# Latent attention unrolled over four head pairs, with the next pair's projections inside the second pass and the outputs taken by halves

## The reference

```python
q = (_rmsnorm(c_q, q_norm) @ w_uq).reshape(B, L, MLA_HEADS, MLA_QK_DIM)          # rank 256 -> 8 x (64 + 32)
q = jnp.concatenate([q[..., :64], _rope(q[..., 64:], cos, sin)], axis=-1)
kv = (_rmsnorm(c_kv, kv_norm) @ w_ukv).reshape(B, L, MLA_HEADS, 64 + 64)          # rank 128
k_nope, mv = kv[..., :64], kv[..., 64:]
k_rope = _rope(k_r[:, :, None, :], cos, sin)                                      # one for all heads
k = jnp.concatenate([k_nope, jnp.broadcast_to(k_rope, (B, L, MLA_HEADS, 32))], axis=-1)
mla = _block_sweep(q, k, mv, 96 ** -0.5, ..., mla_mask)                           # softmax(q k) v, chunk-causal
mla = mla.reshape(B, L, MLA_WIDTH) * jax.nn.silu(m_gate)
y = jnp.concatenate([fox, mla], axis=-1) @ w_out
```

## Time and profile before

| | |
|---|---|
| runs, median of 3 (lowest to highest) | 3171.92 us (3170.37 to 3172.45) |
| the profiled execution | 3178.12 us, its span 3176.3 us |
| TensorE busy | 3044.0 us, 96% of the span |
| VectorE, ScalarE, GpSimd busy | 1526.0, 947.3, 762.2 us |
| mean granted clock of TensorE | 0.975 |
| stages LAT and MLA | 2620.3 to 3064.2 us of the span |

### The profile page before, as it was taken

One profiled execution on the slowest core, in us unless ns is written; L12 is line 12 of the kernel. 1 busy time (PEld: TensorE's weight loads), 2 busy tenths in 40 slices (PEclk: granted clock), 3 DMA queues, 4 the chain that ended last, 5 costly groups with the idle time before them and its releaser, 6 DMA issues.

```text
span 3176.3 us, 38630 instructions
## 1 busy us (share of the span) xinstructions
PE 3044.0 (96%) x14225; PEld 2339.0 (74%) x14225; DVE 1526.0 (48%) x1761; ACT 947.3 (30%) x1502; POOL 762.2 (24%) x486
## 2 busy tenths in 40 slices
PE   6999999999999999999999999999999999999998
PEld 5887875556777777778888888777777777666666
DVE  6464554555344343453344334441455554566654
ACT  4323235666200022322221122221143431333441
POOL 5302112223233312133333333312110101101025
PEclk8999999999999999999999999999899999999999
DMA  5201000000211101011111111102100001000023
GB/s 199 67 21 34 28 21 14 14 14 18 85 50 43 49 28 34 21 47 47 46 46 46 46 46 48 51 30 84 28 21 15 8 11 30 5 2 7 1 100 119
DMA packets 162998, 128.83 MB, mean 41 GB/s; under 512 B 14880, under 2 KB 146688, under 8 KB 162608
## 3 DMA queue, kind: packets, MB, share of 16 engines
q1 hardware_dynamic: 161456, 118.55, 12.3%
q10 hardware_dynamic: 1408, 8.50, 0.7%
HBM read 114.20 MB, written 12.65 MB: 40 GB/s over the span
## 4 chain that ended last, share of the span: by engine, by line
PE 66%; DVE 5%; issue 2%; ACT 1%; DMA 1%; SPq 0%; POOL 0%; DVEq 0%; ACTq 0%; POOLq 0%
PE ps L675 16%; PE ps L677 15%; PE ps L676 15%; PE ps L2345 7%; PE ps L594 2%; PE ps L2404 2%; PE ps L2405 1%; PE ps L2406 1%; PE ps L2489 1%; PE ps L2491 1%; PE ps L2490 1%; PE ps L671 1%; DVE dF L1883 1%; PE ps L612 1%; PE ps L2302 0%
## 5 line engine op out<-in xcount | busy, mean ns | idle before, releaser
L675 PE MATMUL ps<-NH,w_high 128*128 128x512 f32 (+1 forms) x2048 | 801.8, 391 | 31.3 <-POOL w_low L962 8.0
L676 PE MATMUL ps<-NL,w_high 128*128 128x512 f32 (+1 forms) x2048 | 802.7, 392 | 0.0
L677 PE MATMUL ps<-NH,w_low 128*128 128x512 f32 (+1 forms) x2048 | 799.0, 390 | 0.0
L960 POOL CAST w_high<-w_raw 128x1024 fp32r<-128x1024 f32 x193 | 212.1, 1099 | 2233.3 <-PE ps L677 1203.7
L962 POOL TENSOR_TENSOR w_low<-w_raw,w_high 128x1024 fp32r<-128x1024 f32 x193 | 485.0, 2513 | 15.4
L675 PEld LDWEIGHTS ps<-NH,w_high 128*128 128x128 f32 x2048 | 389.9, 190 | 129.8 <-issue 25.7
L677 PEld LDWEIGHTS ps<-NH,w_low 128*128 128x128 f32 x2048 | 390.4, 191 | 85.0
L676 PEld LDWEIGHTS ps<-NL,w_high 128*128 128x128 f32 x2048 | 389.6, 190 | 85.7
L737 DVE TENSOR_TENSOR hT<-hT,ps 128x1024 f32<-128x1024 f32 x168 | 205.1, 1221 | 250.1 <-PE ps L677 250.1
L1306 ACT ACTIVATE probs_high<-ps 128x512 fp32r<-128x512 f32 (+4 forms) x224 | 112.8, 504 | 228.5 <-PE ps L2345 189.6
L1851 DVE TENSOR_TENSOR probs_low<-probs,probs_high 128x512 fp32r<-128x512 f32 (+4 forms) x224 | 133.2, 599 | 86.5 <-ACT probs L1308 81.7
(11 more groups left out here) (355 smaller groups left out, 5108.2 us busy)
## 6 DMA issues: line engine op xcount, KB each, us to landing
w_raw<-in_w_in SPq DMA_DIRECT2D x69, 512.0 KB, 3.8
w_raw<-in_w_up SPq DMA_DIRECT2D x44, 512.0 KB, 3.8
w_raw<-in_w_out SPq DMA_DIRECT2D x24, 512.0 KB, 3.5
w_raw<-in_w_down SPq DMA_DIRECT2D x22, 512.0 KB, 3.7
w_raw<-in_w_xkv SPq DMA_DIRECT2D x8, 512.0 KB, 5.9
x_in<-in_x SPq DMA_DIRECT2D x8, 512.0 KB, 9.3
residual_spill<-hT SPq DMA_DIRECT2D x1, 4096.0 KB, 13.6
hT<-residual_spill ACTq DMA_DIRECT2D x1, 4096.0 KB, 13.0
```

What stands on the lines that cost most here:

```text
L675: nc.tensor.matmul(o, wh, xh, start=start, stop=False)
L676: nc.tensor.matmul(o, wh, xl, start=False, stop=False)
L677: return nc.tensor.matmul(o, wl, xh, start=False, stop=stop)
L960: nc.gpsimd.tensor_copy(WH[slot][:, :], w_raw[slot][:, :]).then_inc(w_high, 1)
```

## The change

- The loop over MLA is written out: four pairs in the program, no loop; the order has no units for the values of the meta tokens (`pair_order(False)`, 56 units).
- A pair's projections are packed over its two heads into five jobs (`m_project`): QN (queries without rope, 64 + 64 rows, 12 matmuls), QP (rope part and its half-swapped copy, 12), KN (keys, 6), KVM (meta keys and meta values), VN (values by tokens: the latent is the stationary operand, 8 x 3 matmuls of 128 columns; no transposes). They use one pair of banks (`SP_`); both heads' outputs use the other (`SU`).
- The next pair's jobs are issued within the second pass, ahead of blocks 1, 6, 10, 16 and 21 (`M_JOB`). ScalarE's high parts follow its exponentials 3, 10, 12 and 18 (`M_HIGH`), VectorE's rotation stands at 8 and 9, its low parts at 3, 4, 11 to 14 and 19. The values are split after the second pass and in the next first pass. Queries and keys have two sets of buffers in `NH` and `NL`; their constant rows are filled once by GpSimd, ahead of the split of pair 1's first tile.
- Numerators and denominators are taken by head and half (after blocks 9, 17, 23 and the last), the reciprocal by quarters of 256 columns (`m_invert`: two at blocks 24 and 26, two in the next first pass), the product by halves (`m_finish`).
- Of the 61 + 4 x 64 fillers of LAT and MLA none is left; the 50 ahead of OUT stay.
- LAT projects the query latents first, then keys and values, then the rope key; the sums and rows of the norms lie between matmuls of the later projections (`between`), with their own buffers; the rotated key is made behind the norms. The rope table is loaded without a wait for the last FOX pair.
- SP loads a pair's weights in 4 + 8 parts in place of 4 + 4.

```diff
-            st_mla = Stage(st_nkvm, 2, list("xwxwxoo") * 2, 116, 4)
+            st_mla = Stage(st_nkvm, 4, [], MLA_UNITS, 2)
...
+        M_JOB = {1: QN, 6: QP, 10: KN, 16: KVM, 21: VN}
+        M_HIGH = {3: QN, 10: QP, 12: KN, 18: KVM}
+        M_ROTATION = {8: 0, 9: 1}
+        M_LOW = {3: [(QN, 0)], 4: [(QN, 1)], 11: [(QP, 0)], 12: [(QP, 1)], 13: [(KN, 0)], 14: [(KN, 1)], 19: [(KVM, 0), (KVM, 1)]}
+        M_TAKEN = {9: (0, 0), 17: (0, 1), 23: (1, 0)}
...
+            dense(pe, LAT, 0, 0, 0, NH, NL)
+            dense(pe, LAT, 0, 1, 1, NH, NL)
+            wait_bank(pe, LAT, 0, 0)
+            dense(pe, LAT, 0, 2, 2, NH, NL, meta=(bank[LAT.bank(0)], 0, l_meta), between={
+                (0, 4): lambda: norm_sums(pe, "q", 0), (HALF, 0): lambda: norm_sums(pe, "q", 1),
+                (HALF, 6): lambda: norm_rows(pe, "q")})
+            dense(pe, LAT, 0, 3, 3, NH, NL, between={
+                (0, 4): lambda: norm_sums(pe, "kv", 0), (HALF, 1): rope_meta, (HALF, 3): lambda: norm_rows(pe, "kv"),
+                (HALF, 6): lambda: norm_sums(pe, "kvm", 0)})
...
+            m_project(0, QN)
+            norm_rows(pe, "kvm")
+            for j in (QP, KN, KVM, VN):
+                m_project(0, j)
+            for pm in range(4):
+                pb, s = pm + 4, pm % 2
+                pe.wait_ge(m_qk, pm + 1)
...
+                    elif what[0] == "p2":
+                        _, h, half, j, n, unit = what
+                        if pm < 3 and n in M_JOB:
+                            m_project(pm + 1, M_JOB[n])
+                        pe.wait_ge(p_rows[h], pb * 32 + 32)
+                        wait_bank(pe, MLA, pm, unit)
...
+            def m_project(pm, j):
+                o = m_slot(pm, j)
...
+                else:
+                    for t in range(NT):
+                        ts = slice(t * P, (t + 1) * P)
+                        mm = three(o[:, ts], kvH[:, 0, ts], kvL[:, 0, ts], WH[s1][:, late], WL[s1][:, late], True, True)
+                    mm.then_inc(tile_done, 1)
...
+            def m_denominators(pm, h, half):
+                hs = slice(half * HALF, (half + 1) * HALF)
+                dve.wait_ge(p_pv, (pm + 4) * 28 + 14 * h + (14 if half else 5) + 4)
+                nc.vector.tensor_copy(dF[HD * h:HD * h + HD, hs], pair[SU][HD * (1 - h):HD * (1 - h) + HD, hs]).then_inc(m_den, 1)
+            def m_invert(pm, quarter):
+                qs = slice(quarter * 256, (quarter + 1) * 256)
+                dve.wait_ge(m_den, 4 * pm + 3 + quarter // 2)
+                nc.vector.reciprocal(dF[:, qs], dF[:, qs]).then_inc(m_rec, 1)
...
+                    elif what[0] == "p2":
+                        n = what[4]
+                        if n in M_TAKEN:
+                            m_denominators(pm, *M_TAKEN[n])
+                        if n in (24, 26):
+                            m_invert(pm, (n - 24) // 2)
+                        if n == 27:
+                            m_finish(pm, 0)
...
+                        if pm and seen in (2, 4):
+                            m_invert(pm - 1, 2 + seen // 4)
+                        if pm and seen == 6:
+                            m_finish(pm - 1, 1)
+                        if seen == 8:
+                            m_values_low(pm)
```

More of the change, by code:

```diff
@@ L191, in pair_order @@
         out.append(("pv", 1) + blocks[m % 14] + (m,))
-    assert unit == 58
+    assert unit == (58 if metas else 56)
     return out
 LAG = 3
+MLA_UNITS = 56
+QN, QP, KN, KVM, VN = range(5)
 ROWS = 126
@@ L615, in norm_pe @@
             mm.then_inc(n_row, 1)
-            if name in UPDATED:
-                busy(bank[1], 14)
         def norm_dve(dve, name):
@@ L993, in _, with one @@
                         nc.gpsimd.tensor_copy(spH[n % 3][:, c0:HALF], xS[n % 4][:, c0:HALF]).then_inc(s_hi, 1)
-            tiles(ahead + 12, NTILES)
+            third = MLA.w0 + 2
+            def one(n):
+                pool.wait_ge(w_landed[n % 2], 16 * (n // 2 + 1))
+                pool.wait_ge(tile_done, n - 1)
+                split(n % 2, n)
+            assert third % 2 == 1
+            tiles(ahead + 12, third - 1)
+            one(third - 1)
+            pool.wait_ge(tile_done, LAT.tile(0, 4))
+            pool.wait_ge(w_ready, third)
+            for s_ in range(2):
+                for h in range(2):
+                    for n, (to, value) in enumerate(((KH, 1.0), (KL, 0.0), (QH, 0.0), (QL, 0.0))):
+                        pool.wait_ge(m_filled, 8 * s_ + 4 * h + n) if s_ + h + n else None
+                        nc.gpsimd.memset(to[s_][h][96:P, :].bitcast(F32), value).then_inc(m_filled, 1)
+            pool.wait_ge(m_filled, 16)
+            one(third)
+            tiles(third + 1, NTILES)
             if NTILES % 2:
@@ new lines, in latent @@
+            def latent(k, c):
+                wait_done(act, LAT, 0, k)
+                nc.scalar.activation(lat[:, c, 0:T], pair[LAT.slot(k)], ACT.Copy).then_inc(job_free[LAT.slot(k)], 1)
+            act.wait_ge(p_pv, 4 * 28 + 4)
+            latent(0, 0)
+            act.wait_ge(p_o, 5)
+            wait_freed(act, LAT, 0, 0)
+            norm_square(act, "q", 0)
+            latent(1, 1)
+            wait_freed(act, LAT, 0, 1)
+            norm_square(act, "q", 1)
+            norm_std(act, "q")
@@ new lines, in _ @@
+            latent(2, 2)
+            act.wait_ge(l_meta, 1)
+            nc.scalar.activation(lat[:, 2, T:T + META], bank[LAT.bank(0)][:, 0:META], ACT.Copy).then_inc(l_mfree, 1)
+            wait_freed(act, LAT, 0, 2)
+            norm_square(act, "kv", 0)
+            for c in range(2):
+                norm_high(act, "q", c)
+            norm_std(act, "kv")
+            act.wait_ge(l_mfree, 1)
+            norm_square(act, "kvm", 0)
+            norm_high(act, "kv", 0)
+            norm_std(act, "kvm")
@@ new lines, in k_rope @@
+            def k_rope(src, done, lo, n, parts, free):
+                done()
+                nc.vector.tensor_tensor(parts[0][0:32, 0:n], src[0:32, 0:n], rope_m[0:32, lo:lo + n], ALU.mult)
+                nc.vector.tensor_tensor(parts[1][0:32, 0:n], src[HD:96, 0:n], rope_m[HD:96, lo:lo + n], ALU.mult)\
+                    .then_inc(free, 1)
+            dve.wait_ge(rope2_in, 48)
+            dve.wait_ge(n_lo, NORM["kvm"][2] + 1)
+            k_rope(pair[LAT.slot(3)], lambda: wait_done(dve, LAT, 0, 3), 0, T, ud, job_free[LAT.slot(3)])
@@ L2431, in _ @@
                               m_own, m_ownT, J + 3, J + 4, ready, 8)
-            for x in range(4):
-                if x < 2:
-                    wait_bank(pe, LAT, 0, x)
-                dense(pe, LAT, 0, x, x, NH, NL, meta=(bank[LAT.bank(x)], 0, unit_done) if x < 2 else None)
-            for name, n in (("q", 24), ("kv", 15), ("kvm", 22)):
-                norm_pe(pe, name)
-                wait_pair(pe, MLA, 0, 0)
-                busy(pair[MLA.slot(0)][:, 0:HALF], n)
-            pe.wait_ge(n_lo, NORM["kvm"][2] + 1)
@@ new lines, in rope_meta @@
+            def rope_meta():
+                slot = (LAT.w0 + 3) % 2
+                pe.wait_ge(l_mfree, 1)
+                for c in range(C):
+                    mm = three(bank[LAT.bank(0)][:, 0:META], WH[slot][:, c * P:(c + 1) * P], WL[slot][:, c * P:(c + 1) * P],
+                               NH[:, c, T:T + META], NL[:, c, T:T + META], c == 0, c == C - 1)
+                mm.then_inc(unit_done, 1)
+            dense(pe, LAT, 0, 0, 0, NH, NL)
+            dense(pe, LAT, 0, 1, 1, NH, NL)
```

568 lines of the change are left out of this document (389 added, 179 removed).

## The result

The changed kernel takes 3124.4 us (median of 4 runs, 3116.2 to 3126.4) against 3172.2 us of the kernel before, run beside it (4 runs, 3170.4 to 3176.2). The ratio is 0.9843, 95% interval 0.9823 to 0.9863: faster by 1.6%, 47.8 us. The forecast was 3117 us, 55 us faster, with a range of 3098 to 3141.

The account below looks back on a forecast made before the run. VectorE was taken to bound the interlude between pairs (25.97 of 27.7 us), TensorE the second pass. Savings of 35.3 (periods) + 1 (last pair) + 19 (latents and pair 0) = 55 us gave 3171.9 - 55 = 3117 us, range 3098 to 3141.

Parts of the forecast that it names:

- (c): Rival: recurring waits hold TensorE at 1.2 GHz through the three second passes; slower, up to 3266 us; chance 0.05.
- (b): Rival: stalls and clock loss at their upper ends, period 84.5 us, prologue saving 14; 30 saved, 3142 us; chance 0.17.
- Second pass: Second pass with the next pair's projections inside: 39.5 + 10.3 = 49.8 us, before stalls and splits.
- The projections: Next pair's five jobs on TensorE in the second pass: 10.3 us added.
- The stalls: Second pass: TensorE waits from inserted VectorE and ScalarE steps, at masked blocks and reciprocal quarters; 2 us (nothing to 5).
- the splits: GpSimd weight splits in second passes of pairs 0, 1 and 2, blocking VectorE's low parts: 2.5 us each pass (1 to 5).
- First pass: First pass stays 21.7 us (18.5 to 24): VectorE's lag replaces the clock's 3.5 us loss.
- The period: From first pass to first pass: 21.7 + 49.8 + 2 + 2.5 + 2 = 78.0 us; 35.3 saved over three.
- Pair 3: Last pair, no projections and no split in its way: 21.7 + 39.5 + 1 = 62.2 us against 63.2, 1 saved.
- Latents and pair 0: Stretch before pair 0's first pass: projections end at 62 us, pass starts at about 90; 19 us saved (12 to 25).
- The loop's turn: Unrolling saves the loop's turn inside the second period: 3 us, already counted in the 269.3.
- The constants on GpSimd: GpSimd's 16 constant fills before pair 0: 1 us each, hidden.

Follow-up runs that it names:

- Run 1: Changed kernel with the next pair's projections and their splitting behind the second pass instead of inside it: 3167.3 us, ratio 0.9984 to the kernel before.
- run 4: Changed kernel plus fillers at blocks 23 to 26 of the second pass, ahead of four early first-pass units and ahead of block 0: 3119.7 us, ratio 0.9834.
- 9: Changed kernel without reciprocal quarters 0 and 1 and half 0's product in the second pass's tail (output incomplete): 3110.0 us, ratio 0.9798.
- run 2: Changed kernel with the query norm's row and the other two norms' sums and rows behind the latent projections: 3131.7 us, ratio 0.9864.
- 7: Changed kernel with the 16-column matmuls spread three by three over the first pass, not in one run at its start: 3117.4 us, ratio 0.9824.
- 6: Changed kernel plus one 512-column filler ahead of each three 16-column matmuls opening the first pass: 3134.8 us, ratio 0.9874.
- 11: Changed kernel plus fillers only at blocks 23 to 26 of the second pass, pairs 0 to 2: 3117.2 us, ratio 0.9815.
- 5: Changed kernel with reciprocal quarters 2 and 3 and half 1's product late in the next first pass, behind maxima 18 to 20: 3116.8 us, ratio 0.9825.
- 10: Changed kernel without reciprocal quarters 2 and 3 and half 1's product in the next first pass (output incomplete): 3116.6 us, ratio 0.982.
- the candidate: Changed kernel plus fillers before pair 0, in the second pass's tail and ahead of block 0, and reciprocal quarters 2 and 3 late: 3111.3 us, ratio 0.9807.

## Why the prediction was right, and which terms were off

**Direction, range and mechanism: right.** The interlude was VectorE's chain and is hidden in the second pass; the passes had the room. Run 1 shows it by itself. None of the rivals came about: no second pass shows a clock under 0.96, which speaks against (c), and the time lies between the forecast and (b). How near the sum came is in part luck, as the next paragraphs show: several terms were off and made up for each other.

**Second pass: right to half a us on average, by errors that cancel.** Forecast 54.3; measured 55.4, 54.8 and 53.9 (from start to start of their first matmuls). The projections cost what was forecast, 10.4 us against 10.3 (QN 2.8, QP 2.9, KN 1.4, KVM 0.5 and VN 2.8). The stalls were 2.6 to 3.1 us instead of 2, the splits 1 instead of 2.5. And a term was missing: in pair 2, which has no splits, 39.5 + 10.4 + 2.6 makes 52.5 of the 53.9 us. The other 1.4 us lie between the pass's own matmuls, in steps under 0.1 us each. The stalls are where they were forecast, ended by low parts: 0.66 us at the masked blocks, 0.64 ahead of KVM, 1.44 at the quarters (0.86 in pair 2). VectorE is busy 35.5 us without splits and 38.6 with them (36.3 forecast), ScalarE 33.0 (33.1); over pair 1's period VectorE is busy 54.8 us, as said.

**The splits: over-priced.** Pair 2's second pass holds none, since the loads of the output's tiles stand behind pair 3's rows of maxima in SP's queue: I had put them into pairs 0, 1 and 2, and two of those hold them. And two cost 1 us (54.8 against 53.9), not 2.5. The lock is there; GpSimd's timeline in pair 1, VectorE's beside it, and the same two low parts in pair 2, with GpSimd idle:

```profile
2841.24 2.71 POOL L1016 TENSOR_TENSOR w_low<-w_raw,w_high 128x1024 fp32r<-128x1024 f32 x1
```

```profile
2839.36 2.34 DVE L2185 TENSOR_TENSOR probs_low<-probs,probs_high 128x128 fp32r<-128x128 f32 x3
...
2842.23 2.47 DVE L2185 TENSOR_TENSOR probs_low<-probs,probs_high 128x384 fp32r<-128x384 f32 x2
```

```profile
2923.44 0.98 DVE L2185 TENSOR_TENSOR probs_low<-probs,probs_high 128x384 fp32r<-128x384 f32 x2
```

Two low parts that take 0.98 us alone take 2.47 and end behind the GpSimd step's end at 2843.95, as in the earlier trace rows. But the splits come at blocks 16 to 21, under the long blocks and the projections, where by the forecast's estimate 1.8 us of delay is hidden; the reading of pair 3, whose splits hit short blocks, did not carry over. By the rule of the Trainium skill, "SBUF — State Buffer", section "SBUF: two separate sides", the later of the two instructions is blocked fully, and the trace agrees; what that costs the pass depends on the slack there, 1 us here against 2.1 in pair 3 of before.

**First pass: the step that failed.** I wrote that "the clock's loss is replaced by VectorE's lag" and took 21.7 us, with 2 us more for the clock over the period. Measured: 25.3, 25.6 and 26.9 us, of which the clock takes 9.0, 6.2 and 8.5. Pulling the two apart: VectorE's lag costs hardly anything (rest 18.0 us without the quarters, 18.6 with them, 18.1 in the kernel before), while the clock's loss did not go away but grew, in pairs 1 to 3 from 4.0 to 6.2 us on average (6.6 in the changed kernel's own trace). A lag of some 3 us that did not come stood in for most of a clock's loss that did; that the sum of the two was off by only 2 us is luck. The reading of before was short too: its loss was taken as 3.5 us, as in pairs 0, 1 and 3, and pair 2 lost 5.1. The period came out at 80.5 us instead of 78.0, nearly all of it in the first pass, 7.6 us over the three. Rival (b) forecast a clock's loss of this kind, but its reason, the three idle pieces per pair, is not shown: runs 4 and 9 have falls without them.

**Pair 3: 4.7 us off, by the clock and by two splits.** Its first pass took 23.3 us (5.1 lost to the clock, not a lag), its second 43.7 against 41.6 in the earlier trace rows, where a lowered stretch takes 1.7 of the difference. I had taken 39.5 for it, as if the two splits of before were gone, and they are not: 2.1 us of the 4.7.

**Latents and pair 0: right.** 60.8 us to the end of the projections (62 forecast), 29.2 more to the first pass (28), TensorE idle 12.8 us in these (17). That the norms between the matmuls pay is shown by run 2. The loop's turn, put at 3 us, made its interlude 1.8 to 2.2 us longer than the others of the earlier trace rows; the sum takes it from the measured 269.3 either way. The constants on GpSimd took 0.95 us each for 16 and delayed nothing, as taken. 21.4 us saved against 19.

**What brings the clock down is not settled.** Shown: a fall needs no idle time within the first pass, and none in the tail before it (run 4, pair 3); it needs neither the narrow matmuls at the pass's start (7) nor a lack of wide ones among them (6). With the tail's quarters gone half of the loss is gone (9), with the tail filled a quarter (11). The four changes to the tail and the quarters (5, 9, 10, 11) average 3.4 to 4.6 us lost against 6.2, and the candidate, which joins the late quarters and the fillers, 1.7. But a single pass varies by up to 3.4 us with little or nothing changed (5.1 and 8.5 in two pairs of one trace, 3.4 and 5.1 for pair 3 in two traces of the same code), so the means of three passes from one profile each rank the runs only roughly. What remains of the loss in run 9, with no wait over 0.3 us in the last blocks, has no cause shown here.

## What to carry to other kernels

A chain of one engine between two passes of another can be hidden by issuing the next item's work inside the pass, a step at a time; it pays if each inserted step is shorter than what the pass's look-ahead covers, and by the waits seen here (up to 0.86 us) the places to avoid are the short blocks at the end. When a pass starts behind waits, read its length as work and clock apart (length less the clock's loss) in several traces before blaming the engine that is late: here the lag was blamed and the clock was it. And put work that nobody waits for, such as a finished pair's division, at a pass's end and not among its first or the previous one's last steps: the traces speak for it (runs 5 and 9), though only with the candidate did the whole time get near to showing it.

## What the runs showed of the hardware

- The granted clock stood at 0.50 for 10.2 us of pair 2's first pass with TensorE busy all of the time, and behind a tail whose longest wait was 0.86 us. Its second passes held 1.00 with 3.1 us of idle time in pieces of 0.2 to 0.9 us.
- Fillers did not reliably hold it up: in run 4 it fell with TensorE busy all through the 14.1 us before and the 6.8 us of the stretch itself.
- VectorE's two low parts of 128x384 took 2.47 us beside a GpSimd subtraction and 0.98 us without one. Its copy out of an accumulator (128 partitions' matmul results, 64x512) took 0.68 us beside the same subtraction and 0.69 without: not held up.
- Of these fp32 matmuls, each with a stationary operand of its own, one of 16 columns takes as long as one of 128: each follows the one before by 0.11 us at the full clock and by 0.21 at the low one (16 columns in the rows above, 128 in VN before pair 0). One of 256 columns takes hardly longer (0.12 us at the full clock, at the end of pair 2's second pass), one of 384 takes 0.18.
- A reciprocal costs VectorE 1.75 us for 128x256, against 6.56 us for 128x1024 in one: cutting it in quarters costs 0.4 us.
